# Causal branch of a three-branch decoder step: one slot more from scores to transposes, a fourth score buffer, fillers at other slots

## The reference: what is computed

```python
def diff_attend(q, k, v, q_pos, k_pos, lam, lam_init, g_subln, slopes):
    s = jnp.einsum('bqhcd,bkhcd->bhcqk', q, k).astype(jnp.float32) * (A_DQK ** -0.5)
    dist = (q_pos[:, None] - k_pos[None, :]).astype(jnp.float32)
    s = s - (slopes[:, None, None, None] * dist[None, None])[None]
    s = jnp.where(dist >= 0, s, NEG_INF)
    p = jax.nn.softmax(s, axis=-1)
    a = p[:, :, 0] - lam * p[:, :, 1]
    o = jnp.einsum('bhqk,bkhe->bqhe', a.astype(v.dtype), v)
    return rms_norm(o, g_subln) * (1.0 - lam_init)
```

## Time and profile before

| what | us |
|---|---|
| median of three runs | 651.28 |
| profiled execution | 648.06 |
| its span, first to last instruction | 646.4 |
| matmul engine busy | 613.4 |
| VectorE busy | 324.9 |
| ScalarE busy | 280.8 |
| GpSimd busy | 97.4 |

### The profile page before, as it was taken

One profiled execution on the slowest core, in us unless ns is written; L12 is line 12 of the kernel. 1 busy time (PEld: TensorE's weight loads), 2 busy tenths in 40 slices (PEclk: granted clock), 3 DMA queues, 4 the chain that ended last, 5 costly groups with the idle time before them and its releaser, 6 DMA issues.

```text
span 646.4 us, 12429 instructions
## 1 busy us (share of the span) xinstructions
PE 613.4 (95%) x5110; PEld 573.6 (89%) x5110; DVE 324.9 (50%) x677; ACT 280.8 (43%) x551; POOL 97.4 (15%) x182
## 2 busy tenths in 40 slices
PE   2899999899999999999999999999999999999996
PEld 1899999788999999999887875679999999999896
DVE  3942113875435857557474545456445244254334
ACT  4854344565455243246545445456322323221132
POOL 2010100000013316567122222101000000000000
PEclk9999999999999999999999999999999999999999
DMA  8653433220248847775421534233532242322103
GB/s 267 235 171 124 162 134 100 66 66 2 66 125 267 267 141 238 214 244 166 143 92 42 176 101 163 65 97 123 173 102 95 67 129 67 112 85 66 33 3 130
DMA packets 58744, 82.73 MB, mean 128 GB/s; under 512 B 4592, under 2 KB 48160, under 8 KB 58432
## 3 DMA queue, kind: packets, MB, share of 16 engines
q1 hardware_dynamic: 49808, 55.58, 26.5%
q0 software_dynamic: 8880, 26.36, 13.5%
HBM read 74.68 MB, written 7.24 MB: 127 GB/s over the span
## 4 chain that ended last, share of the span: by engine, by line
PE 84%; DVE 6%; DMA 4%; ACT 3%; issue 2%; POOL 1%; SPq 0%; DVEq 0%; ACTq 0%; POOLq 0%
PE pj L707 18%; PE pj L708 18%; PE pj L709 18%; PE pj L1051 3%; PE pj L1053 3%; PE pj L1052 3%; PE pt_bank L819 3%; DMA out<-stage 3%; DVE w_lo L1392 2%; DMA w_raw<-in_w_mem_kv 2%; PE ps L707 2%; PE ps L708 2%; PE ps L709 2%; PE ps L718 1%; PE po_bank L856 1%
## 5 line engine op out<-in xcount | busy, mean ns | idle before, releaser
L707 PE MATMUL pj<-xh,w_hi 128*128 128x260 f32 x1024 | 293.7, 287 | 0.4 <-ACT gate L1141 0.4
L708 PE MATMUL pj<-xh,w_lo 128*128 128x260 f32 x1024 | 289.1, 282 | 0.0
L709 PE MATMUL pj<-xl,w_hi 128*128 128x260 f32 x1024 | 288.9, 282 | 0.0
L707 PEld LDWEIGHTS pj<-xh,w_hi 128*128 128x128 f32 x1024 | 192.8, 188 | 9.8 <-issue 8.0
L708 PEld LDWEIGHTS pj<-xh,w_lo 128*128 128x128 f32 x1024 | 192.8, 188 | 0.2
L709 PEld LDWEIGHTS pj<-xl,w_hi 128*128 128x128 f32 x1024 | 192.8, 188 | 0.0
L1392 DVE TENSOR_TENSOR w_lo<-w_raw,w_hi 128x1024 fp32r<-128x1024 f32 x84 | 99.7, 1221 | 160.3 <-ACT w_hi L1078 160.3
L1078 ACT ACTIVATE w_hi<-w_raw 128x1024 fp32r<-128x1024 f32 x84 | 84.7, 1049 | 24.5 <-PE pj L1053 22.7
L1141 ACT ACTIVATE gate<-pj 128x260 f32<-128x260 f32 x44 | 16.9, 386 | 70.9 <-PE pj L709 70.9
L1141 ACT ACTIVATE region<-pj 128x260 f32<-128x260 f32 x44 | 17.0, 387 | 67.7 <-PE pj L709 67.5
L1051 PE MATMUL pj<-w_hi,mixh 128*128 128x256 f32 (+1 forms) x160 | 45.0, 281 | 1.2 <-DVE w_lo L1392 0.8
(11 more groups left out here) (276 smaller groups left out, 894.0 us busy)
## 6 DMA issues: line engine op xcount, KB each, us to landing
w_raw<-in_w_in SPq DMA_DIRECT2D x64, 512.0 KB, 4.4
ring<-in_cache_diff_kv POOLq DMA_DIRECT2D x32, 256.0 KB, 3.5
out<-stage SPq DMA_DIRECT2D x19, 256.0 KB
ring<-in_cache_mem_kv POOLq DMA_DIRECT2D x16, 256.0 KB, 3.6
w_raw<-in_w_out SPq DMA_DIRECT2D x8, 512.0 KB, 4.0
w_raw<-in_w_mem_kv SPq DMA_DIRECT2D x4, 512.0 KB, 10.1
region<-in_x_prompt SPq DMA_DIRECT2D x4, 512.0 KB, 11.8
q_all<-q_rows POOLq DMA_DIRECT2D x8, 256.0 KB, 3.7
```

The source lines that it names most:

```text
L707: pe.matmul(out, wh, mh, start=(i == 0), stop=False)
L708: pe.matmul(out, wl, mh, start=False, stop=False)
L709: last = pe.matmul(out, wh, ml, start=False, stop=(i == n - 1))
```

## The change

Branch A gets one slot more between normalising and transposing: the transposes of unit s-3 and the value products of unit s-4 now stand in slot s, and the loops run one slot longer (slots 0 to 19 on the matmul engine). The new table `TURNED` holds 3 for A and 2 for B and M, whose loops keep their numbers. ScalarE's `copy_probs` and its copies of finished heads move one slot with them; `normalise` stays at s-1. A fourth score buffer is `prod`. The fillers, which stood in slots 0, 1, 3, 5, ..., 15, 16, 17, 18, stand in 0, 1, 2, 4, 6, ..., 14, 16, 17, 18. The splits follow their fillers: high halves in slots 4, 5, 12, 13, 18, 19 in place of 5, 6, 13, 14, 18, 19, and low halves in 5, 6, 13, 14, 19, 19 in place of 6, 7, 14, 15, 18, 18.

```diff
@@ -196,7 +196,7 @@
         g_row = ring[:, 0, :, :].rearrange("p a b -> p (a b)")
         g_row_m = ring[:, 1, :, :].rearrange("p a b -> p (a b)")
 
-        sc = {"A": [work[:, 1024 * i:1024 * i + 1024] for i in range(3)],
+        sc = {"A": [work[:, 1024 * i:1024 * i + 1024] for i in range(3)] + [prod[:, :]],
               "B": [work[:, 768 * i:768 * i + 768] for i in range(3)]}
         pt = {"A": [work[:, 3072 + 512 * i:3584 + 512 * i] for i in range(2)],
               "B": [work[:, 2304 + 768 * i:3072 + 768 * i] for i in range(2)]}
@@ -478,8 +478,8 @@
 
 
 
-        SLOTS = {"A": [0, 1, 3, 5, 7, 9, 11, 13, 15, 16, 17, 18], "BM": [1, 3, 5, 7, 9, 11, 13, 15, 17, 20, 22, 24]}
-        LAST_SLOT = {"A": OA_UNITS + 2, "BM": OB_UNITS + OM_UNITS + 2}
+        SLOTS = {"A": [0, 1, 2, 4, 6, 8, 10, 12, 14, 16, 17, 18], "BM": [1, 3, 5, 7, 9, 11, 13, 15, 17, 20, 22, 24]}
+        LAST_SLOT = {"A": OA_UNITS + 3, "BM": OB_UNITS + OM_UNITS + 2}
         FILL, SPLIT, SPLIT_LO = {}, {}, {}
         for which, n0 in (("A", N_A), ("BM", N_BM)):
             FILL[which] = {s: (n0 + i // 4, i % 4) for i, s in enumerate(SLOTS[which])}
@@ -681,6 +681,7 @@
             return max(0, v // 2 if v <= OB_UNITS else v - OB_UNITS // 2)
 
         RANGES = {"A": (0, OA_UNITS), "BM": (OA_UNITS, NU)}
+        TURNED = {"A": 3, "BM": 2}
 
         @block.tensor
         def _(pe):
@@ -816,7 +817,7 @@
                 blocks = {"A": q + 1, "B": 6, "M": 4}[br]
                 for k in range(blocks):
                     dst = pt_bank[:, 128 * k:128 * k + 128] if k < 4 else po_bank[:, 128 * k - 512:128 * k - 384]
-                    last = pe.transpose(dst, sc[br][u % 3][:, 128 * k:128 * k + 128], ident[:, :])
+                    last = pe.transpose(dst, sc[br][u % len(sc[br])][:, 128 * k:128 * k + 128], ident[:, :])
                 last.then_inc(s_T, 1)
 
             def values_pair(u):
@@ -867,7 +868,8 @@
 
             def attention(which):
                 a, b = RANGES[which]
-                for s in range(a, b + 3):
+                late = TURNED[which]
+                for s in range(a, b + late + 1):
                     if s < b:
                         scores(s)
                     if which == "BM" and s == a + 1:
@@ -878,14 +880,14 @@
                         project_unit(*FILL[which][s - a])
                     if sample_first:
                         sample_values(NK + s - a - 3)
-                    if a <= s - 3:
-                        values(s - 3)
+                    if a <= s - late - 1:
+                        values(s - late - 1)
                     if which == "BM" and s >= a + 3 and not sample_first:
                         sample_values(NK + s - a - 3)
                     if s - a in FILL[which] and not unit_first:
                         project_unit(*FILL[which][s - a])
-                    if a <= s - 2 < b:
-                        transposes(s - 2)
+                    if a <= s - late < b:
+                        transposes(s - late)
 
             sa = s_a.rearrange("p (t r) -> p t r", t=2)
             smt = s_m.rearrange("p (t r) -> p t r", t=2)
@@ -1171,7 +1173,7 @@
                 br, p, q = attn_slot(u)
                 act.wait_ge(s_nm, u + 1)
                 k4 = 2 * (u % 4)
-                buf = sc[br][u % 3]
+                buf = sc[br][u % len(sc[br])]
                 if br == "A":
                     kn = 128 * (q + 1)
                     act.activation(buf[:, 0:kn], buf[:, 0:kn], ACT.Exp, bias=nm[:, k4:k4 + 1],
@@ -1203,22 +1205,23 @@
 
             def attention(which):
                 a, b = RANGES[which]
-                for s in range(a, b + 4):
-                    v = s - 4
+                turned = TURNED[which]
+                for s in range(a, b + turned + 2):
+                    v = s - turned - 2
                     if which == "A" and a <= v < b and attn_slot(v)[2] == QT - 1:
                         h = attn_slot(v)[1]
                         act.wait_ge(s_pv, v + 1)
                         act.activation(oraw[:, h, 0:T], po_bank[:, :], ACT.Copy).then_inc(s_oe, 1)
                     fill = FILL[which].get(s - a)
                     late = fill or (which == "BM" and s < a + OB_UNITS)
-                    if a <= s - 2 < b and not late:
-                        copy_probs(s - 2)
+                    if a <= s - turned < b and not late:
+                        copy_probs(s - turned)
                     if s < b:
                         exps(s)
                     if fill:
                         evacuate_unit(*fill)
-                    if a <= s - 2 < b and late:
-                        copy_probs(s - 2)
+                    if a <= s - turned < b and late:
+                        copy_probs(s - turned)
                     for n, half in SPLIT[which].get(s - a, ()):
                         hi_split(n, (half,))
 
@@ -1479,9 +1482,10 @@
 
                 br, p, q = attn_slot(u)
                 dve.wait_ge(s_S, u + 1)
-                if u >= 3:
-                    dve.wait_ge(s_T, u - 2)
-                buf, S, k4 = sc[br][u % 3], ps[u % 2], 2 * (u % 4)
+                deep = len(sc[br])
+                if u >= deep:
+                    dve.wait_ge(s_T, u - deep + 1)
+                buf, S, k4 = sc[br][u % deep], ps[u % 2], 2 * (u % 4)
                 if br == "A":
                     kn = 128 * (q + 1)
                     for c in range(2):
@@ -1510,7 +1514,7 @@
             def normalise(u):
 
                 br, p, q = attn_slot(u)
-                buf, k4 = sc[br][u % 3], 2 * (u % 4)
+                buf, k4 = sc[br][u % len(sc[br])], 2 * (u % 4)
                 n = 1 if br == "B" else 2
                 dve.wait_ge(s_ex, u + 1)
                 link(dve.reciprocal(rs[:, k4:k4 + n], sm[:, k4:k4 + n]))
@@ -1541,7 +1545,7 @@
 
             def attention(which):
                 a, b = RANGES[which]
-                for s in range(a, b + 3):
+                for s in range(a, b + TURNED[which] + 1):
                     if a <= s - 3 and (which == "A" or s >= a + OB_UNITS + 3):
                         gate_output(s - 3)
                     if s < b:
```

## The result

The changed kernel took 646.50 us in the median of five runs (646.02 to 648.37), the kernel before 651.28 (649.12 to 652.70): a ratio of 0.9932 with a 95% interval of 0.9906 to 0.9959. Run again beside 31 executions of the kernel before it took 647.49 in the median of ten against 649.89, ratio 0.9954 (0.9934 to 0.9974). The ratios here are the recorded ones; they are not quotients of the two medians. It is faster by about half a per cent, 2.4 to 4.8 us, where 1.6 had been forecast. The profiled execution took 646.02, 2.04 less than that of before.

The account below looks back on a forecast made before the run. PE, busy 95% of 646.4 us, was taken to bound the kernel. The terms -1.88 - 0.91 + 0.2 + 0.05 + 0.92 = -1.62 us, laid on the median 651.28, gave 649.6, range 647.2 to 652.6.

Parts of the forecast that it names:

- What bounds the kernel, and why PE waits: Whole kernel, then causal branch: PE 95% busy; its two waits, 2.79 us, come from ScalarE's copies late behind wide exponentials.
- The first wait: Ahead of unit 1's value products, slot 4 before, slot 5 after: 1.88 us shrinks to 0.2, bounds 0 and 0.9.
- The second wait, the splits: Unit 5's value products: wait of 0.91 us goes to 0; weight splits one slot earlier cost 0.05 in slots 7 and 15.
- The end: Slots 18 and 19: last value products come right behind their transposes, 0.92 us bare, bounds 0.75 and 1.0.
- depth is what was missing: Rival, causal branch: extra depth removes both waits and covers the end, -2.79 us, so 648.5; chance 17%.
- The fourth buffer and later transposes: Causal branch: fourth score buffer and transposes one slot later bring no new wait and remove none, 0 us.
- The branch's sum: Causal branch: all terms together shorten it by 1.62 us.
- The sum: Whole kernel: the terms' -1.62 us carried over to the runs' median of 651.28, giving 649.7, stated as 649.6.
- the depth rival: Rival, causal branch: a want of depth caused both waits; -2.79 us, so 648.5; chance 17%.
- the wait only moves: Rival: unit 1's value products wait 0.9 to 1.9 us in slot 5, the end takes 0.92; middle 650.8; chance 18%.
- every value product waits: Rival, slots 5 to 15: value products in six odd slots without filler wait 0.91 each; +3.6 us, 654.9; chance 7%.

Follow-up runs that it names:

- e5: Kernel before with VectorE's long operation low_a one slot earlier, in slot 1; 648.51 us, ratio 0.9980 to the kernel before.
- e1: Kernel before with only branch A's fillers moved to the new slots; 646.66 us, ratio 0.9938 to the kernel before.
- e2: Changed kernel with the fillers back at the old slots, keeping the extra depth; 651.94 us, ratio 1.0032 to the kernel before.
- e3: Kernel before against itself, with no edit; 650.63 us, ratio 1.0015.
- e6: Kernel before with one more VectorE operation of low_a's size in slot 2, result unused; 653.03 us, ratio 1.0039 to the kernel before.
- e7: Changed kernel with two more VectorE operations of low_a's size in slot 2, results unused; 651.54 us, ratio 1.0015 to the kernel before.

## Why the prediction was wrong

The mechanism held, and most terms did; the sum was carried from one execution to all of them, and that failed.

- *What bounds the kernel, and why PE waits.* Right. e5 moved VectorE's operation away and the first wait shrank with it. That the split of weights does the same for the second wait was not tested by itself.
- *The first wait.* I laid out copy 1 for 129.14 and a wait of 0.12, taken as 0.2. The changed branch began 0.43 earlier; with that added, copy 1 stands at 129.25. Measured wait 0.19.
- *The second wait, the splits.* 0 and 0.05 forecast; v5 starts 0.55 behind sc9 and v3 0.89 behind sc7, which is what these scores take, so both are 0.
- *The end.* 0.92 forecast, 1.29 - 0.36 = 0.93 measured. Right, and so "depth is what was missing" was rightly not the forecast; e1 and e2 settle it.
- *The fourth buffer and later transposes.* "0" was not quite right: e1 and the changed kernel differ by 0.42 while the end costs 0.93, so 0.51 is won inside the branch by the extra slot. In the old filler slots depth costs 1.42, which "no new wait" would have missed.
- *The branch's sum.* -1.62 forecast, 65.36 - 67.38 = -2.02 measured. The other 0.4 lies in hand-overs that I left alone: score groups followed by a filler take 0.48 and 0.72 (1 and 3 blocks) where followed by value products they took 0.54 and 0.75, 0.29 in all, and the transposes 0.13 less than counted.
- *The step that failed* is "The sum", where -1.62 was laid on the median, as if an idle 1.88 us cost 1.88 us. In the execution that I read it did. In others the clock then falls, and 1.49 us more are lost (e3), 1.46 (e6), 1.5 (e7). The removal of the wait gives that back as well. If each low mean clock, 26 of 72 executions before and none of 15 after, stood for one such fall, it would be worth about 0.36 x 1.5 = 0.54 in the mean. An estimate from these rows: 2.02 + 0.54 = 2.6 us. The means of all executions, 650.39 (72) and 647.28 (15), differ by 3.1. With the clock at 0.998 or more they differ by 2.65, so the clock, wherever it fell, accounts for some 0.5 of the 3.1 and the branch of the profiled execution for 2.0. The remaining 0.6 is open: it is there with a full clock too. Whether the change also alters how often the clock falls in the second attention isn't shown. Groups of five to 31 executions of one kernel differ in their means by as much (646.86 and 647.49 for the changed one, 650.17 to 651.10 for the one before).
- *The sign that I passed over* stood in the text: the profiled execution lay 3.2 under the median of the runs. Something in the other executions cost time (the clock only a part of it: those with 0.998 or more still have a mean of 649.24, 1.2 above the profiled one), and I carried the difference over as if it were the same for both kernels. The profiled execution of the changed kernel lies only 0.5 under its median.
- *The range and the chances.* The lower end, 647.2, allowed for the depth rival and scatter, not for a second price on the wait. It also doesn't follow from the numbers given for it: the depth rival's 648.5 less the scatter of 1.6 is 646.9, and 646.50 lies below that too. The repeat's 647.49 lies inside the range, so the scatter of the first five executions has its part in the miss. A gain of over 0.5% had 12%; the measured 0.46 to 0.68% says it deserved about half. The rivals "the wait only moves" and "every value product waits" did not occur.

The fastest arrangement tried is the simplest one: fillers at the new slots without the extra slot and buffer has the shortest branch, though its time can't be told from the changed kernel's.

## What to carry to other kernels

A profile is one execution: where it lies well away from the median of the runs, ask what the others have that it lacks before a term is carried over. A wait of the matmul engine is priced with what it can do to the clock behind it, so two microseconds of idle time can be worth more than they last. When a copy stands late in a queue, look first at what stands ahead of it there: moving other work by one slot did here what more depth and one more buffer did not.

## What the runs showed of the hardware

The granted clock fell to its lower level behind idle times of 1.88 (e3), 3.01 (e6) and 1.76 us (e7) in a dense stretch of matmuls, and matmuls of 260 columns listed at 0.28 us then took 0.42 for some 3 to 4 us. Yet it stayed at 1.00 behind the same 1.88 us in the first profiled execution, and behind 2.56 us in e2. Behind 0.74 and 0.9 us (e5) it stayed at 1.00 as well. So the length of the wait alone doesn't decide it, and what else does is open. The counts of low mean clocks, which take in falls at other places, don't settle it: 1 of 11 with a wait of 0.74, 26 of 72 with 1.88, 9 of 12 with 3.01, but 4 of 12 with 2.56 (e2), 8 of 12 with 1.76 (e7) and 2 of 10 with none (e1). The Trainium skill (TensorE: Matmul & The Clock Gate, section "A second HAM failure mode: psum-queue depth-cycling") tells of a kernel in which frequent short idle times between groups of matmuls make the clock swing between its two levels, and of throughput lost by it. These runs agree in kind, with about 1.5 us for each fall, but here single idle times did it.
